# HGRN2 values as seven half-size products with channels on partitions, turned into rows, in place of products by rows

## What is computed

```python
proj = h @ p["w_in"]                                    # h: 384 x 1024
(hg_q, hg_f_fwd, hg_f_bwd, hg_v, hg_g, ...) = _split(proj[..., D_CONV:], PLAIN_SPLITS)
o_hg, s_hg = _scan_both_directions(
    _hgrn2_chunked, (heads(jax.nn.silu(hg_q), HG_DK), heads(hg_v, HG_DV)), ...)
```

## Time and profile before

| | us |
|---|---|
| median of 3 runs | 1387.83 (1387.24 to 1388.75) |
| the profiled execution | 1387.85 |
| its span, first to last instruction | 1386.0 |
| TensorE busy in the span | 1346.9 (97%) |
| DVE, ACT, POOL busy | 608.4, 387.8, 327.4 |
| mean granted TensorE clock | 0.997 of full speed |

### The profile page before, as it was taken

How to read it: one execution, slowest core, us unless ns; L and a number is a source line. 1 busy time by engine, 2 the same in 40 slices (tenths; PEclk the granted TensorE clock), 3 DMA queues, 4 the chain that set the end, 5 groups by cost and what they waited for, 6 DMA issues and landing times.

```text
span 1386.0 us, 20777 instructions
## 1 busy us (share of the span) xinstructions
PE 1346.9 (97%) x7728; PEld 945.7 (68%) x7728; DVE 608.4 (44%) x1349; ACT 387.8 (28%) x772; POOL 327.4 (24%) x260
## 2 busy tenths in 40 slices
PE   7999999999999999999999999999999999999996
PEld 2695899899988996788988875444454445444452
DVE  3467452885545476433431375332223322322224
ACT  3232222322554354323421241221122212211122
POOL 0431234243134553544433001000000000000001
PEclk9999999999999999999999999999999999999998
DMA  9640423133212437721335437999999999999992
GB/s 361 209 133 2 137 92 122 52 101 94 90 61 92 125 104 302 261 62 31 104 95 168 134 122 283 405 417 420 419 419 421 421 420 421 420 418 420 420 416 82
DMA packets 109457, 321.42 MB, mean 232 GB/s; under 512 B 12457, under 2 KB 72361, under 8 KB 80848
## 3 DMA queue, kind: packets, MB, share of 16 engines
q1 hardware_dynamic: 98128, 307.51, 58.0%
q0 software_dynamic: 2560, 8.81, 1.6%
q10 hardware_dynamic: 8704, 4.20, 1.2%
HBM read 319.94 MB, written 4.33 MB: 234 GB/s over the span
## 4 chain that ended last, share of the span: by engine, by line
PE 83%; DMA 11%; DVE 3%; ACT 1%; POOL 1%; issue 1%; SPq 0%; DVEq 0%; POOLq 0%
PE banks L653 24%; PE banks L620 17%; PE banks L2942 12%; DMA w<-in_exp_w 9%; PE banks L2989 7%; PE banks L2844 5%; PE banks L1060 3%; PE banks L2829 2%; PE banks L1198 1%; PE banks L2837 1%; DMA ring<-in_ada_w 1%; PE banks L627 1%; PE banks L893 1%; PE banks L772 1%; PE banks L704 1%; PE banks L1257 1%
## 5 line engine op out<-in xcount | busy, mean ns | idle before, releaser
L2942 PE MATMUL banks<-w,xg 128*64 128x512 f32 (+1 forms) x1312 | 236.0, 594 | 2.4 <-DMA w<-in_exp_w 2.4
L2942 PEld LDWEIGHTS banks<-w,xg 128*64 128x64 f32 (+1 forms) x1312 | 72.0, 126 | 151.6 <-issue 126.1
L653 PE MATMUL banks<-hT,ring 128*128 128x192 f32 x888 | 154.4, 326 | 0.2 <-DMA ring<-in_w_in 0.2
L653 PEld LDWEIGHTS banks<-hT,ring 128*128 128x128 f32 x888 | 145.3, 190 | 2.2 <-DMA ring<-in_w_in 0.8
L3319 POOL DMA_INDIRECT fetched<-token_rows,row_of_place x32 | 32.1, 1004 | 443.7 <-DVE row_of_place L3120 433.6
L2989 PE MATMUL banks<-w,hidT 128*64 128x512 f32 (+1 forms) x656 | 122.5, 600 | 0.2
L2844 PE MATMUL banks<-y,selT 128*128 128x512 f32 x384 | 115.0, 415 | 0.0
L653 PE MATMUL banks<-x,ring 128*128 128x192 f32 x592 | 108.7, 327 | 0.9 <-ACT late L1376 0.9
L653 PE MATMUL banks<-x,combos 128*128 128x192 f32 x592 | 108.4, 326 | 0.7 <-ACT late L1369 0.7
L653 PEld LDWEIGHTS banks<-x,combos 128*128 128x128 f32 x592 | 98.1, 190 | 1.0 <-POOL ring L2494 0.9
L653 PEld LDWEIGHTS banks<-x,ring 128*128 128x128 f32 x592 | 97.4, 190 | 1.4 <-ACT late L1376 1.2
(11 more groups left out here) (499 smaller groups left out, 2028.3 us busy)
## 6 DMA issues: line engine op xcount, KB each, us to landing
w<-in_exp_w SPq DMA_DIRECT2D x198, 1024.0 KB, 13.9
ring<-in_w_in SPq DMA_DIRECT2D x46, 1024.0 KB, 5.4
ring<-in_ada_w SPq DMA_DIRECT2D x24, 1024.0 KB, 7.2
ring<-in_w_branch SPq DMA_DIRECT2D x8, 1024.0 KB, 6.3
ring<-in_w_out SPq DMA_DIRECT2D x4, 1024.0 KB, 6.7
arena<-in_sh_w SPq DMA_DIRECT2D x3, 1024.0 KB, 8.4
x<-in_x_sample SPq DMA_DIRECT2D x4, 512.0 KB, 8.9
token_rows<-whole_rows SPq DMA_DIRECT2D x3, 384.0 KB, 20.1
```

Source lines behind the costliest of these rows:

```text
L653: last = mm(out, lhsT=w[:, k, :], rhs=tokens[:, k, :], start=start and k == 0, stop=k == KD // 2 - 1, skip_group_check=not start)
L2942: ins = mm(ps[lo:hi, :], lhsT=xg[:, k, a_ * P + lo:a_ * P + hi], rhs=w13[:, a_, u, :, k, :], start=k == 0, stop=k == KD - 1)
```

## The change

`hg_v` joins the list of pairs, between the forget gates and `hg_g`. Its sums are built with channels on partitions in `hmix`, a buffer that the levels use later. After `hg_g` 0, TensorE turns the four 128x128 tiles of each token tile (3 x 4 transposes) into a bank, and ACT copies them into `hv`. On ACT the four kept copies of each `hg_v` pair come in the queue before those of `hg_g`; on DVE the addition of pair `hg_v` d stands at the head of direction d's work on the forget gates; on POOL, by the list, the combinations of `hg_v` come before the clearing of `hattn` and the sum of the keys.

```diff
-        PAIRS = [(name, h) for name in PAIRED[0:2] + FORGET + ("hg_g",) for h in range(2)] + \
+        PAIRS = [(name, h) for name in PAIRED[0:2] + FORGET + ("hg_v", "hg_g") for h in range(2)] + \
@@ block_sums
+            if name[0] == "hg_v":
+                return hmix[:, 2 * name[1]:2 * name[1] + 2, :]
@@ tensor
             for name in FORGET:
                 for h in range(2):
                     pair(name, h)
-            project_N("hg_v", "act")
             for h in range(2):
-                pair("hg_g", h)
+                pair("hg_v", h)
+            pair("hg_g", 0)
+            banks.emptied(pe, ("hg_v", 1, "y"))
+            for t in range(NT):
+                flip4(("hv", t), "act", [hmix[:, c, tok[t]] for c in range(CW)])
+            pair("hg_g", 1)
@@ scalar: block_sums_free
-                if name[0] in ("hg_g", "gdn_g"):
+                if name[0] in ("hg_v", "hg_g", "gdn_g"):
                     return
@@ scalar
+            for h in range(2):
+                keep_all("hg_v", h)
+            keep_all("hg_g", 0)
             for t in range(NT):
-                copy(hv[:, t, :], ("hg_v", t))
-            for h in range(2):
-                keep_all("hg_g", h)
+                copy(hv[:, t, :], ("hv", t))
+            keep_all("hg_g", 1)
@@ vector
             for d in range(2):
+                add_up("hg_v", d)
                 dve.wait_ge(s_forget.sem, 4 * d + 4)
                 for c in range(CW):
```

## The result

The changed kernel takes 1397.24 us (median of 6 runs, 1396.74 to 1399.54), the kernel before in the same session 1387.91 (6 runs, 1387.24 to 1390.37). The ratio is 1.0068, 95% interval 1.0055 to 1.0081: slower by 0.7%, 9.3 us by the medians. The forecast was 1399.2 with a range of 1395.4 to 1401.8. An experiment's edit can move these by a few lines.

What follows compares the result with a forecast made beforehand. The prediction took TensorE, busy 97% of the span, to bound the kernel. Wait 9.0, own work 0.1 and clock 2.2 us make 11.3, on 1387.85 giving 1399.2 us; range 1395.4 to 1401.8.

Steps and rivals of the forecast that it cites:

- The wait of 9.0 us: TensorE waits 9.0 us before the second product of `hg_g` 0, for POOL's combination queued behind the late key sum.
- The clock: TensorE's clock falls during the wait, so work just behind it is slow: 2.2 us, bounds 0 and 3.0.
- One to one to the end: A delay or gain of TensorE around `hg_v` reaches the kernel's end in full, with no idle time to absorb it.
- the term for the turning: The 12 added transposes on TensorE: 24 records at 0.109 us, 2.62 us, making TensorE's own work +0.10 us.
- The draw in streamed columns: TensorE streams 12288 columns before and after; the transposes give back all that the pairs save.
- with 1.3 us to spare: On DVE, direction 0's 5.66 us and some 1.9 us of the `hg_v` 1 addition fit before 211.85, 1.3 us left.
- POOL's eight combinations: The added `hg_v` combinations cost POOL 10 us but would fit in its 14.28 us idle before the key sum.
- the rival of the longer wait: DVE late with direction 0 beside POOL's work: wait 10.8 us, full clock price 3.0, 1401.8 us; chance 0.07.
- The low bound of the wait, 7.5: TensorE's wait at `hg_g` 0 if POOL's first combination (L2478) ran at 1.26 us instead of 2.78.
- the one given back later: Some of the later 7.5 us of TensorE idle time (454 to 760 us) shrinks: 1395.4 us; chance 0.04.
- The one with no clock loss: TensorE waits at `hg_g` 0 but its clock stays full: 1397.0 us; chance 0.12.
- The "not slower" rival: Direction 1's keys ready for POOL's sum by 206.2 instead of 215.2, only +0.10 us left: 1388.0 us; chance 0.06.

Runs made afterwards that it cites:

- the filled wait: Changed kernel with 24 unread products of 128x192 put into TensorE's 9.06 us wait before the second product of `hg_g` 0: 1395.02 us.
- two experiments: Changed kernel with one addition alone moved later on DVE: `hg_v` 1 behind both directions' work, 1398.20 us; `hg_v` 0 behind direction 0's work, 1399.79 us.
- the first repair: Changed kernel with both additions of `hg_v` on DVE moved behind the forget-gate work of both directions: 1390.61 us.
- the repairs: Changed kernel with `hg_v` additions behind the forget gates (1390.61 us), with `hg_g` 0's combinations ahead of POOL's key sum (1389.49 us), or with both (1386.53 us).

## Why the prediction was right, point by point

**Direction and size** were right: slower, 9.3 us by the medians against 11.3. The measured time lies inside the range.

**The wait of 9.0 us** came at the named place, on the named combination, and took 9.06. The clock came with it, and the filled wait shows that it is the clock: 1.98 in the profile against 2.2, or 1.74 against the products at full clock. That the size is so near is in part luck: behind the waits of 8.0 and 9.1 us of two experiments the same six products lost 3.0 and 2.5 us on that measure, up to the bound of 3.0. "One to one to the end" held: +9.91 in the stretch against +9.3 at the medians, the rest being differences between runs (the profiled run of the changed kernel reached the stretch 1.15 us earlier than that of before, so the spans differ by 8.9).

**The step that was off is the term for the turning**: "The 16 records of L627 take 1.75 us, 0.109 each", and then 24 records for 12 transposes. The rule of two records holds for the products; a transpose is one record. The 16 records in the earlier trace rows are those of four banks of four tiles, 16 transposes. So it cost 1.31 us, not 2.62, and TensorE's own work fell by 1.21 us instead of rising by 0.10. That is 1.3 of the 2.0 us by which the forecast was too high. The draw in streamed columns was an error of the same origin: it counts a column of a transpose like one of a product, which has two records.

**A reason that was too narrow**: that direction 1 is late because of the addition of `hg_v` 1. It would have been as late through that of `hg_v` 0. I had fitted direction 0's work into its slot "with 1.3 us to spare"; the trace shows none. One scaling took 2.74 us, so direction 0 took 7.98 us (201.95 to 209.93) instead of 5.66, and the first three operations of the addition took 0.84 (209.93 to 210.77) instead of the 1.9 in the prediction. The 2.3 us too few in the one were met by the 1.3 us to spare and the 1.1 too many in the other. So the slot was just long enough, and the sum came out right, by luck.

**A cost put at nothing that is not nothing**: POOL's eight combinations. For the sum I looked at whether POOL had time, not at what DVE does beside it. Only the rival of the longer wait named this, and through the wrong operation: the product with the queries of direction 0 kept its 1.76 us, a scaling was what slowed. In the changed kernel this is hidden by the longer wait. In the first repair it is what stays: the keys are 6 us late and TensorE waits 2.7. The low bound of the wait, 7.5, and the 1.5 us named for a case without contention left out a part too: the key sum itself takes 4.01 us beside the product of DVE and 3.43 where DVE is nearly quiet.

**The rivals.** The longer wait and the one given back later did not come. The one with no clock loss was refuted by the windows. The "not slower" rival named its point rightly, a key sum ready by 206: the repairs reach the same by another way, by taking the sum out from between TensorE and its combination.

## What to carry to other kernels

When work is moved into a queue that another engine feeds, look at what stands behind the first instruction that waits for that engine, and ask whether it needs to stand there; here one reordering of GpSimd's queue took 11.0 us out of the stretch, and the change, good for 1.1 there, was hidden under it (in the kernel's time that gain is at the edge of what the runs tell). A wait on TensorE costs more than its length once the clock falls behind it. A kernel that leaves a step out computes with other values: see whether later work depends on them before its time is read. And count a transpose's records before pricing it by those of a product.

## What the runs showed of the hardware

- VectorE operations with one SBUF tensor that start beside a GpSimd operation slow down to about its length: 128x384 scalings took 0.41 to 0.47 us alone, 1.42 to 1.43 beside a combination of 1.27 to 1.38, 2.74 beside a combination and the clearing in a row. One that had begun before kept its length: the floor L2031, 128x1536, took 0.95 us from 213.92 with the key sum starting at 214.15. So did the additions with an operand in PSUM: L1842 took 0.34 us at 214.21 in the first experiment, beside a combination that ran from 212.63 to 215.40.
- Behind waits of TensorE of 2.0 and 2.7 us the clock fell in two profiles (9.72 us for the six products behind the wait, 1.7 more than the 8.04 at full clock) and did not in a third with 2.7 us. Behind unfilled waits of 8.0 to 9.1 us the clock was low in all three profiles, for 1.7 to 3.0 us more than the 8.04.
- A float32 transpose of 128x128 costs 0.109 us in a row of them and is one record; a float32 product of 128x192 is two records and 0.325 us.
